# Normalisation stage: shift and scale weights loaded and multiplied ahead of the tokens, gate columns between the token groups, normalised rows written by POOL

## The chip, the cores and the metric

The kernel runs on one core of a Trainium2 chip. The metric is the device time of one execution in microseconds (us); lower is better. A time that is given is the median of several executions.

## The reference

The kernel computes two layers of a hybrid mixer over 1024 latent tokens and 256 context tokens of width 1024. The change touches only the head of each layer, the modulated layer norm:

```
shift, scale, gate = jnp.split(mod[:, None, :], 3, axis=-1)
shift_c, scale_c, gate_c = jnp.split(mod_c, 3, axis=-1)
u = _layer_norm(h) * (1.0 + scale) + shift
uc = _layer_norm(hc) * (1.0 + scale_c) + shift_c
z, xbc, dtr, q, k, v, gd, hp, gh = jnp.split(u @ w_in, IN_SPLITS, axis=-1)
```

Here `mod` and `mod_c` are rows of 3072 numbers, SiLU of a conditioning vector of 1024 times `w_ada` (1024 x 3072, fp32) plus a bias. Their first 1024 columns are the shift, the next the scale, the last the gate. The gate is only used at the layer's end, in the output stage. The rest of a layer (projections, a state-space scan, differential attention, long convolutions, the output projection with its own layer norm) stands after this stage and uses `u` and `uc`.

## The kernel before

`hybrid_backbone` runs its stages one after the other, and twice, once for each layer: `norm_stage`, `v_dt_stage`, `project_stage` and so on. Between two stages stands a barrier of all engines, so a stage ends with the last work of its slowest engine, and nothing of one stage lies beside another. Inside a stage each engine has a program of its own, written out by hand, and the order in it is fixed. Engines meet through semaphores.

`norm_stage` must leave two copies of the modulated and transposed tokens in SBUF: `u_hi`, rounded to fp32r, and `u_lo`, the remainder. Each is 128 partitions x 8 column blocks (k) x 1280 tokens. The tokens come as 10 tiles of 128 (2 of context, then 8 of latent tokens) in three groups: `batches` holds 2, 4 and 4 tiles. Item n is one column block of one group, 8 items for each group, 24 in all.

- SP (L204 to L221) issues all DMAs: the two conditioning vectors, all the tokens (`xn`: 1 MB, then twice 2 MB), the bias, and then `w_ada` in six column groups j of 512 columns, 2 MB each, into the two slots of `wa`. From j = 2 on it first waits until TensorE has multiplied group j - 2.
- PE (TensorE, L287 to L310) multiplies group j with the two conditioning vectors, 8 matmuls of 512 columns. The order is all six groups, then 16 small transposes that turn the shift and scale rows onto the partitions (`pT`), then the token transposes item by item into four PSUM slots (`px`), four 128 x 128 transposes for an item of 512 tokens.
- DVE (VectorE, L246 to L285) takes the first 6 token tiles through the layer norm (statistics, reciprocal, and the normalised rows by a `tensor_scalar` of 1024 columns, L265), then adds the bias to the six groups (L272), copies `pT` to `modT`, normalises the last 4 tiles, and at the end computes the remainder of each item (L284).
- ACT (ScalarE, L224 to L244) computes the SiLU, a square root for each tile, and then two activations for each item: `u_hi` (L240) and the same values in full fp32, `u` (L243), from which DVE subtracts.
- POOL (GpSimd) does nothing in this stage.

Only when `modT` is there can ACT begin with the items, and `modT` waits for all six groups, those of the gate too:

```
for j in range(NCH):
    pe.wait_ge(wada[j % 2], 16 * (j // 2 + 1))
    if j >= 2:
        pe.wait_ge(mod_ready, j - 1)
...
pe.wait_ge(mod_ready, NCH)
for k in range(2 * KD):
    mm = pe.transpose(pT[:, 2 * k:2 * k + 2], mod[:, k * P:(k + 1) * P], ident[0:2, 0:2])
```

## Time and profile before

| what | value |
|---|---|
| median of 3 runs | 4172.46 us (4168.78 to 4177.13) |
| the profiled execution, its own time | 4166.99 us |
| its span, first to last instruction | 4164.9 us |
| mean granted TensorE clock | 0.928 of full speed |
| busy: PE, DVE, ACT, POOL | 3522.2, 2521.2, 1081.6, 699.4 us |
| norm stage of layer 0, first DMA issue to last DVE work | 4.49 to 116.88 us |
| norm stage of layer 1, the same | 2228.86 to 2339.60 us |

The rows below are of four views. The timeline gives the start, the length, the engine, the line and the tiles of an instruction, and in brackets the idle time before it and what ended it. The table of windows gives a stretch, its length, the busy time of PE, PEld (weight loads), DVE, ACT and POOL in it, each with its number of instructions, then the granted TensorE clock (PEclk, 1.00 is 2.4 GHz and 0.50 is 1.2 GHz), the share of the DMA engines and their GB/s. The table of lines gives the number of instructions, their busy time in sum and the mean of one in ns. The table of DMA issues gives the count, the size and the us from issue to landing. Names that begin with `l_n_` belong to the norm stage of either layer.

### The profile page before, as it was taken

How to read it: one execution, taken by the hardware profiler on the slowest of the kernel's cores; microseconds unless marked ns; L12 is line 12 of the kernel's file. 1: busy time of each engine (PE TensorE's matmuls, PEld its weight loads, DVE VectorE, ACT ScalarE, POOL GpSimd, SP SyncE). 2: the span in 40 equal slices, each digit the busy share in tenths (PEclk: the TensorE clock that was granted, in tenths of full speed). 3: DMA queues.
4: the chain of work that ended last, by engine and by line, in shares of the span. 5: the costliest groups of instructions: out<-in, count | busy, mean ns of one | idle time of the engine just before them, and what ended most of it. 6: DMA issues, size and time to landing. Idle time of an engine off the chain costs nothing. (4 is left out here: it accounts for less than half of the span.)

```text
span 4164.9 us, 51062 instructions
## 1 busy us (share of the span) xinstructions
PE 3522.2 (85%) x19424; PEld 2889.8 (69%) x19424; DVE 2521.2 (61%) x5084; ACT 1081.6 (26%) x1861; POOL 699.4 (17%) x444
## 2 busy tenths in 40 slices
PE   5789999999778875996996788999999688859888
PEld 1677888888667774775782566788888577737577
DVE  3125677754279996765553324667773699967544
ACT  2212222222144443332110311222211344423310
POOL 0132333322100001210000122433343000012000
PEclk8899999999888997998998799999999799989999
DMA  4154223232253312334325145223231633123432
GB/s 174 55 142 144 94 85 97 81 101 74 72 162 97 89 35 74 122 98 150 118 81 187 36 115 163 88 81 97 81 100 62 188 84 84 40 100 105 134 115 71
DMA packets 414110, 424.53 MB, mean 102 GB/s; under 512 B 56908, under 2 KB 350540, under 8 KB 412710
## 3 DMA queue, kind: packets, MB, share of 16 engines
q1 hardware_dynamic: 368844, 319.55, 26.5%
q10 hardware_dynamic: 45024, 101.73, 6.9%
q8 instruction: 155, 2.54, 0.3%
q14 instruction: 87, 0.71, 0.1%
HBM read 288.28 MB, written 124.53 MB: 99 GB/s over the span
## 5 line engine op out<-in xcount | busy, mean ns | idle before, releaser
L665 PE MATMUL l_p_acc<-l_u_hi,l_p_w_hi 128*128 128x512 f32 (+1 forms) x2240 | 612.4, 376 | 49.5 <-POOL l_p_w_lo L580 37.0
L665 PE MATMUL l_p_acc<-l_u_hi,l_p_w_lo 128*128 128x512 f32 (+1 forms) x2240 | 593.5, 367 | 0.0
L665 PE MATMUL l_p_acc<-l_u_lo,l_p_w_hi 128*128 128x512 f32 (+1 forms) x2240 | 592.2, 367 | 0.0
L665 PEld LDWEIGHTS l_p_acc<-l_u_hi,l_p_w_hi 128*128 128x128 f32 x2240 | 390.4, 190 | 127.9 <-POOL l_p_w_lo L580 37.5
L665 PEld LDWEIGHTS l_p_acc<-l_u_hi,l_p_w_lo 128*128 128x128 f32 x2240 | 386.0, 189 | 72.4
L665 PEld LDWEIGHTS l_p_acc<-l_u_lo,l_p_w_hi 128*128 128x128 f32 x2240 | 385.8, 189 | 72.3
L578 POOL TENSOR_TENSOR l_p_w_hi<-l_p_wt,l_p_zero 128x1024 fp32r<-128x1024 f32 x104 | 207.7, 1997 | 983.2 <-PE l_p_acc L665 816.2
L1945 POOL TENSOR_TENSOR l_sd_xend<-l_sd_tok,l_sd_mine 128x512 f32<-128x512 f32 x80 | 85.6, 1072 | 1283.0 <-ACT l_sd_tok L1900 1282.2
L1402 PE MATMUL l_at_pS<-l_at_k_hi,l_at_q 128*128 128x512 f32 (+1 forms) x400 | 167.1, 418 | 147.2 <-ACT l_at_prob L1517 113.9
L580 POOL TENSOR_TENSOR l_p_w_lo<-l_p_wt,l_p_w_hi 128x1024 fp32r<-128x1024 f32 x104 | 271.0, 2606 | 8.2
L1586 DVE TENSOR_REDUCE l_at_nmax<-l_at_pS 128x1 f32<-128x1280 f32 (+1 forms) x144 | 197.1, 1369 | 81.7 <-PE l_at_pS L1403 78.7
L1517 ACT ACTIVATE l_at_prob<-l_at_pS,l_at_nmax 128x1280 f32<-128x1280 f32 (+1 forms) x144 | 177.4, 1232 | 249.5 <-DVE l_at_nmax L1586 249.5
L1402 PEld LDWEIGHTS l_at_pS<-l_at_k_hi,l_at_q 128*128 128x128 f32 x400 | 79.6, 199 | 186.3 <-ACT l_at_prob L1517 142.7
L876 DVE TENSOR_SCALAR l_p_cv<-l_p_stg,l_p_taps 128x1281 f32<-128x1281 f32 (+1 forms) x56 | 85.0, 1517 | 192.6 <-ACT l_p_stg L729 192.2
L822 DVE TENSOR_TENSOR l_p_R<-l_p_sw,l_p_rs 128x512 f32<-128x512 f32 x72 | 49.6, 689 | 228.7 <-PE l_p_sw L644 228.7
L1434 PE MATMUL l_at_pO<-l_at_v,l_at_mixT 128*128 128x128 f32 x1312 | 180.5, 299 | 7.6 <-ACT l_at_mixT L1524 4.5
L1434 PEld LDWEIGHTS l_at_pO<-l_at_v,l_at_mixT 128*128 128x128 f32 x1312 | 174.4, 215 | 10.1 <-issue 6.5
L878 DVE SCALAR_TENSOR_TENSOR l_p_cv<-l_p_stg,l_p_taps,l_p_cv 128x1281 f32<-128x1281 f32 (+1 forms) x56 | 150.8, 2692 | 2.0
L1524 ACT ACTIVATE l_at_mixT<-l_at_pT 128x512 f32<-128x512 f32 (+1 forms) x200 | 104.0, 520 | 181.3 <-PE l_at_pT L1418 181.3
L295 PE MATMUL l_n_pm<-l_n_wa,l_n_cond 128*2 128x512 f32 x192 | 88.0, 616 | 68.5 <-DMA l_n_wa<-w_ada 68.5
L1403 PE MATMUL l_at_pS<-l_at_k_lo,l_at_q 128*128 128x512 f32 (+1 forms) x400 | 144.0, 367 | 0.0
L643 PE MATMUL l_p_sw<-l_p_R,l_p_late 128*128 128x128 f32 x528 | 107.4, 286 | 34.0 <-DVEq L815 34.0
(324 smaller groups left out, 7051.2 us busy)
## 6 DMA issues: line engine op xcount, KB each, us to landing
l_p_wt<-w_in SPq DMA_DIRECT2D x104, 512.0 KB, 3.9
l_n_wa<-w_ada SPq DMA_DIRECT2D x12, 2048.0 KB, 8.2
xbc_d<-l_p_fin ACTq DMA_DIRECT2D x32, 640.0 KB, 2.9
kf_d<-l_p_R SPq DMA_DIRECT2D x72, 256.0 KB, 3.6
l_o_oT<-o_d SPq DMA_DIRECT2D x18, 1024.0 KB, 6.7
l_at_K<-kf_d SPq DMA_DIRECT2D x64, 256.0 KB, 2.9
l_o_rows<-w_out SPq DMA_DIRECT2D x32, 512.0 KB, 4.6
qk_d<-l_p_late ACTq DMA_DIRECT2D x12, 1280.0 KB, 4.8
```

The costliest lines, as they stand in the source:

```text
L295: mm = pe.matmul(pm[0:2, (j % 2) * BANK:(j % 2 + 1) * BANK], cond[:, k], wa[:, j % 2, k], start=(k == 0), stop=(k == KD - 1))
L578: pool.tensor_tensor(w_hi[:, m % 2], wt[:, m % 2], zero[:].unsqueeze(2).to_broadcast([P, KD, P]), ALU.add).then_inc(w_rounded, 1)
L580: pool.tensor_tensor(w_lo[:, m % 2], wt[:, m % 2], w_hi[:, m % 2], ALU.subtract).then_inc(w_split, 1)
L643: pe.matmul(out, mats[:, 4 * k + 2 * e], R[:, k, 0, cols], start=True, stop=False)
L665: mm = pe.matmul(acc[:, a:a + w], (w_hi, w_lo)[wp][:, m % 2, k], (u_hi, u_lo)[up][:, k, t0 + c:t0 + c + w], start=(k == n == 0), stop=(k = ...
L878: dve.scalar_tensor_tensor(cv[:, lo:], stg[:, lo:T + 1], taps[:, 0, tile:tile + 1], cv[:, lo:], ALU.mult, ALU.add).then_inc(conv_step, 1)
L1402: pe.matmul(out, q_s[:, s, m, q * P:(q + 1) * P], k_hi[:, s, m, c:c + w], start=True, stop=False)
L1403: mm = pe.matmul(out, q_s[:, s, m, q * P:(q + 1) * P], k_lo[:, s, m, c:c + w], start=False, stop=True)
L1434: mm = pe.matmul(pO[:, 0:P], mixT[:, kt], v_s[:, h % 2, kt], start=(kt == 0), stop=(kt == keys(q) // P - 1))
L1517: act.activation(prob[:, (2 * n + m) % 3, 0:keys(q)], pS[:, m * T:m * T + keys(q)], ACT.Exp, bias=nmax[:, n % 2, m:m + 1], accum_out=sums[ ...
L1524: act.activation(mixT[:, 4 * b:4 * b + w // P].rearrange("p a b -> p (a b)"), pT[:, 0:w], ACT.Copy).then_inc(turned_copied, 1)
L1586: dve.tensor_reduce(nmax[:, n % 2, m:m + 1], pS[:, m * T:m * T + keys(q)], AX.X, ALU.max, negate=True).then_inc(maxed, 1)
```

## The change

The weight loads now come first, and the tokens between them. The first 2 MB group of `w_ada` is loaded in two halves, and there are three weight slots (`WS` = 3) instead of two. The first four groups (`FRONT`, the shift and scale columns) come before the small transposes. Groups 4 and 5, the gate columns, are multiplied between the token groups. The statistics are taken for a whole group of tiles with one square root and one reciprocal, and POOL writes the normalised rows. For the items with odd n, DVE and no longer ACT computes `u` from PSUM (L318).

```diff
+    FRONT = 2 * D // GW
+    WS = 3
...
-                for j in range(NCH):
-                    if j >= 2:
-                        sp.wait_ge(mod_mm, j - 1)
-                    sp.dma_start(wa[:, j % 2], w_ada[:, j * GW:(j + 1) * GW].rearrange("(k p) n -> p k n", p=P)).then_inc(wada[j % 2], 16)
+                load_wada(0)
                 sp.dma_start(ba[:, :], b_ada.partition_broadcast(2)).then_inc(bada, 16)
+                load_wada(1)
+                load_h(0)
+                load_wada(2)
+                load_h(1)
+                load_wada(3)
+                load_h(2)
+                for j in range(FRONT, NCH):
+                    load_wada(j)
...
             @block.scalar
+                def turned(n):
+                    b, k = items[n]
+                    scale, shift = affine(n)
+                    act.wait_ge(xT_ready, n + 1)
+                    act.activation(u_hi[:, k, cols(b)], x_of(n), ACT.Identity, scale=scale, bias=shift).then_inc(hi_ready, 1)
+                    if n % 2 == 0:
+                        if n >= 4:
+                            act.wait_ge(lo_ready, n - 3)
+                        act.activation(u[:, n % 4, 0:width(b)], x_of(n), ACT.Identity, scale=scale, bias=shift).then_inc(u_act, 1)
+                for b, t in enumerate(batches):
+                    act.wait_ge(var_ready, b + 1)
+                    act.activation(mv[:, 2, t[0]:t[-1] + 1], mv[:, 1, t[0]:t[-1] + 1], ACT.Sqrt).then_inc(std_ready, 1)
+                    if b == 1:
+                        act.wait_ge(modT_ready, 1)
+                        for n in range(KD):
+                            turned(n)
+                for n in range(KD, len(items)):
+                    turned(n)
+            @block.gpsimd
+                for b, tiles in enumerate(batches):
+                    pool.wait_ge(rstd_ready, b + 1)
+                    for t in tiles:
+                        pool.tensor_scalar(xn[:, t], xn[:, t], mv[:, 0, t:t + 1], mv[:, 3, t:t + 1], ALU.subtract, ALU.mult).then_inc(xn_ready, 1)
...
             @block.vector
+                def remainders(b):
+                    for n in range(KD * b, KD * (b + 1)):
+                        k = items[n][1]
+                        dve.wait_ge(hi_ready, n + 1)
+                        if n % 2:
+                            scale, shift = affine(n)
+                            dve.tensor_scalar(u[:, n % 4, 0:width(b)], x_of(n), scale, shift, ALU.mult, ALU.add).then_inc(u_dve, 1)
+                            dve.wait_ge(u_dve, n // 2 + 1)
+                        else:
+                            dve.wait_ge(u_act, n // 2 + 1)
+                        dve.tensor_tensor(u_lo[:, k, cols(b)], u[:, n % 4, 0:width(b)], u_hi[:, k, cols(b)], ALU.subtract).then_inc(lo_ready, 1)
+                statistics(0)
                 dve.wait_ge(bada, 16)
+                modulation(0)
+                modulation(1)
+                statistics(1)
+                modulation(2)
+                modulation(3)
                 dve.wait_ge(modT_mm, 1)
                 dve.tensor_copy(modT[:].rearrange("p a b -> p (a b)"), pT[:, 0:4 * KD]).then_inc(modT_ready, 1)
+                dve.wait_ge(modT_ready, 1)
+                remainders(0)
+                statistics(2)
+                modulation(4)
+                remainders(1)
+                modulation(5)
+                remainders(2)
...
             @block.tensor
+                pe.wait_ge(mod_ready, FRONT)
                 for k in range(2 * KD):
                     mm = pe.transpose(pT[:, 2 * k:2 * k + 2], mod[:, k * P:(k + 1) * P], ident[0:2, 0:2])
                 mm.then_inc(modT_mm, 1)
+                turn(0)
+                modulation(4)
+                turn(1)
+                modulation(5)
+                turn(2)
```

SP's queue at the stage's start, before; `l_n_xn` is the tokens, `l_n_wa` the weights:

```order
L209 DMA l_n_xn<-ctx 128x2x1024
L212 DMA l_n_xn<-x 128x4x1024 x2
L213 DMA l_n_ba<-b_ada 2x3072
L218 DMA l_n_wa<-w_ada 128x8x512 x2
L218 DMA l_n_wa<-w_ada 128x8x512 [waits l0_n_mod_mm] x4
```

The same place, now:

```order
L229 DMA l_n_wa<-w_ada 128x4x512
L230 DMA l_n_wa<-w_ada 128x4x512
L243 DMA l_n_ba<-b_ada 2x3072
L232 DMA l_n_wa<-w_ada 128x8x512
L237 DMA l_n_xn<-ctx 128x2x1024
L232 DMA l_n_wa<-w_ada 128x8x512
L237 DMA l_n_xn<-x 128x4x1024
L232 DMA l_n_wa<-w_ada 128x8x512 [waits l0_n_mod_mm]
L237 DMA l_n_xn<-x 128x4x1024
L232 DMA l_n_wa<-w_ada 128x8x512 [waits l0_n_mod_mm] x2
```

5 MB of tokens stood ahead of the first weights; now three weight groups and two token groups stand ahead of the first load that waits for TensorE, and the last 2 MB of tokens behind it.

PE's program around the small transposes (`l_n_pT`), before; `l_n_pm` is a weight group, `l_n_px` an item's transposes:

```order
L295 MATMUL l_n_pm<-l_n_wa,l_n_cond 2x512 [waits l0_n_mod_ready,l0_n_wada1]
L295 MATMUL l_n_pm<-l_n_wa,l_n_cond 2x512 x7
L299 MATMUL l_n_pT<-ident,l_n_mod 128x2 [waits l0_n_mod_ready]
L299 MATMUL l_n_pT<-ident,l_n_mod 128x2 x15
L308 MATMUL l_n_px<-ident,l_n_xn 128x128 [waits l0_n_xn_ready]
```

The same place, now, from the small transposes to the second token group:

```order
L374 MATMUL l_n_pT<-ident,l_n_mod 128x2 [waits l0_n_mod_ready]
L374 MATMUL l_n_pT<-ident,l_n_mod 128x2 x15
L359 MATMUL l_n_px<-ident,l_n_xn 128x128 [waits l0_n_xn_ready]
L359 MATMUL l_n_px<-ident,l_n_xn 128x128 x7
...
L359 MATMUL l_n_px<-ident,l_n_xn 128x128 [waits l0_n_u_dve,l0_n_hi_ready]
L359 MATMUL l_n_px<-ident,l_n_xn 128x128
L348 MATMUL l_n_pm<-l_n_wa,l_n_cond 2x512 [waits l0_n_mod_ready,l0_n_wada1]
L348 MATMUL l_n_pm<-l_n_wa,l_n_cond 2x512 x7
L359 MATMUL l_n_px<-ident,l_n_xn 128x128 [waits l0_n_u_act,l0_n_hi_ready,l0_n_xn_ready]
L359 MATMUL l_n_px<-ident,l_n_xn 128x128 x3
```

Two of the six weight groups moved behind the small transposes, one of them into each gap between token groups, where they hold up the next group's transposes.

## Rows read from the trace of the kernel before

**Rows 1.** Windows, both norm stages: busy us and instructions, clock, DMA
```profile
4.49:116.88 112.39, 66.68 (x192) 22.52 (x192) 44.15 (x91) 33.53 (x61) 0.00 (x0) 0.84 0.45 159
2228.86:2339.60 110.74, 64.22 (x192) 21.68 (x192) 44.16 (x91) 33.53 (x61) 0.00 (x0) 0.73 0.46 162
```

**Rows 2.** Timeline of SP, layer 0: start, us, engine, line, out<-in
```profile
4.49 0.38 SPq L207 DMA_DIRECT2D l_n_cond<-c_ctx  x1
7.82 51.60 SPq L218 DMA_DIRECT2D l_n_wa<-w_ada  x6
```

**Rows 3.** Timeline of TensorE, norm stage of layer 0
```profile
27.36 16.54 PE L295 MATMUL l_n_pm<-l_n_wa,l_n_cond 128*2 128x512 f32 x32 [27.36 <-DMA l_n_wa<-w_ada]
67.61 7.03 PE L295 MATMUL l_n_pm<-l_n_wa,l_n_cond 128*2 128x512 f32 x16 [0.71 <-DMA l_n_wa<-w_ada]
75.41 1.14 PE L299 MATMUL l_n_pT<-ident,l_n_mod 2*128 2x2 f32 x16 [0.77 <-DVE l_n_mod L272]
100.07 1.12 PE L308 MATMUL l_n_px<-ident,l_n_xn 128*128 128x128 f32 x4 [0.22 <-ACT l_n_u L243]
```

**Rows 4.** Timeline of VectorE, norm stage of layer 0
```profile
10.92 1.28 DVE L254 BATCH_NORM_STATS2 l_n_st<-l_n_xn 128x6 f32<-128x512 f32 x2 [10.92 <-DMA l_n_xn<-ctx]
12.24 0.21 DVE L257 BATCH_NORM_AGGREGATE l_n_mv<-l_n_st 128x2 f32<-128x12 f32 x1
37.16 0.68 DVE L272 SCALAR_TENSOR_TENSOR l_n_mod<-l_n_pm,l_n_ba 2x512 f32<-2x512 f32 x1 [8.70 <-PE l_n_pm L295]
74.67 0.68 DVE L272 SCALAR_TENSOR_TENSOR l_n_mod<-l_n_pm,l_n_ba 2x512 f32<-2x512 f32 x1 [7.05 <-PE l_n_pm L295]
116.19 0.69 DVE L284 TENSOR_TENSOR l_u_lo<-l_n_u,l_u_hi 128x512 fp32r<-128x512 f32 x1 [0.65 <-ACT l_n_u L243]
```

**Rows 5.** DMA issues of the stretch 7.7 to 8 us
```profile
l_n_wa<-w_ada SPq DMA_DIRECT2D x1, 2048.0 KB, 19.4
```

**Rows 6.** Timeline of all engines, layer 1, the first weight group
```profile
2251.60 10.74 PE L295 MATMUL l_n_pm<-l_n_wa,l_n_cond 128*2 128x512 f32 x21 [36.17 <-DMA l_n_wa<-w_ada]
2260.31 0.68 DVE L272 SCALAR_TENSOR_TENSOR l_n_mod<-l_n_pm,l_n_ba 2x512 f32<-2x512 f32 x1 [7.60 <-PE l_n_pm L295]
```

**Rows 7.** Timeline of ScalarE, norm stage of layer 0
```profile
87.27 0.55 ACT L240 ACTIVATE l_u_hi<-l_n_px,l_n_modT 128x256 fp32r<-128x256 f32 x1
94.46 0.87 ACT L240 ACTIVATE l_u_hi<-l_n_px,l_n_modT 128x512 fp32r<-128x512 f32 x1
115.01 1.08 ACT L243 ACTIVATE l_n_u<-l_n_px,l_n_modT 128x512 f32<-128x512 f32 x1
```

**Rows 8.** Lines by shape, VectorE: count, busy us and mean ns, idle before
```profile
L284 DVE TENSOR_TENSOR l_u_lo<-l_n_u,l_u_hi 128x256 fp32r<-128x256 f32 x16 | 6.8, 426 | 6.8 <-ACT l_n_u L243 6.8
L764 DVE TENSOR_SCALAR l_p_R<-l_p_sw,l_p_R 64x512 f32<-64x512 f32 x8 | 6.4, 801 | 13.8 <-ACT l_p_R L681 7.4 <-PE l_p_sw L600 4.8 <-ACT l_p_hid L681 1.5
L764 DVE TENSOR_SCALAR l_p_R<-l_p_sw,l_p_R 64x256 f32<-64x256 f32 x2 | 1.1, 534 | 1.5 <-ACT l_p_R L681 0.8 <-ACT l_p_hid L681 0.8
```

**Rows 9.** Windows in the norm stage of layer 1, TensorE's clock
```profile
2302.00:2303.00 1.00, 0.00 (x0) 0.00 (x0) 1.00 (x3) 0.00 (x0) 0.00 (x0) 0.79 0.00 0
2320.00:2322.00 2.00, 1.21 (x8) 0.84 (x8) 1.20 (x2) 2.00 (x5) 0.00 (x0) 1.00 0.00 0
2322.00:2324.00 2.00, 1.00 (x5) 0.49 (x4) 0.88 (x2) 2.00 (x5) 0.00 (x0) 0.77 0.00 0
```

**Rows 10.** Lines by shape, POOL
```profile
L580 POOL TENSOR_TENSOR l_p_w_lo<-l_p_wt,l_p_w_hi 128x1024 fp32r<-128x1024 f32 x104 | 271.0, 2606 | 8.2
L975 POOL CAST l_v_wv_hi<-l_v_wv 128x512 fp32r<-128x512 f32 x16 | 9.8, 613 | 673.5 <-DMA l_v_wv<-w_in 673.5
```

**Rows 11.** Timeline of all engines, projection stage of layer 0
```profile
377.65 0.44 DVE L766 TENSOR_SCALAR l_p_R<-l_p_R 64x512 f32<-64x512 f32 x1
377.89 2.46 POOL L580 TENSOR_TENSOR l_p_w_lo<-l_p_wt,l_p_w_hi 128x1024 fp32r<-128x1024 f32 x1
378.13 2.51 DVE L768 TENSOR_SCALAR l_p_R<-l_p_R 64x512 f32<-64x512 f32 x1
```

155 lines of the change are left out of this document (77 added, 78 removed).

## The prediction

> **What bounds the kernel now.** I read the table of windows first. The two norm stages are 112.4 and 110.7 us long [rows 1], 223 of 4165 us, and in neither is any engine busy for more than 67 us, nor the DMA for more than 0.46 of the time. Barriers stand at both ends, so what such a stage loses in length the kernel loses too. The chain of waits is of no use here, since it shows only the last stage. The timelines show three parts in a row. First, tokens stand ahead of the weights: TensorE starts at 27.36 us [rows 3], though the first DMA was issued at 4.49 [rows 2]. Second, six weight groups pass one by one until the bias of the last at 74.67 [rows 4]. Third, after `modT`, ACT starts at 87.27 behind four normalisations and runs without a pause to the last activation at 115.01 [rows 7]; the last remainder ends at 116.88 [rows 4]. The change goes at all three.
>
> **The loads.** The first MB of tokens is there at 10.92 [rows 4]; the first weight group, 6.29 MB further, lands 19.4 us after 7.82 [rows 2, 5], at 27.2. That is 386 GB/s, 5.4 us for 2 MB. In the new order, with the first half group where the context tokens were, landings would be: first halves 10.9 and 13.6, group 1 at 19.1, context 21.8, group 2 at 27.2, latent tokens 32.7, group 3 at 38.1, latent tokens 43.5, groups 4 and 5 at 49.0 and 54.4. Group 3 is issued once group 0 is multiplied. Behind this wait on SP stand the last tokens and both gate groups. The queue has work up to 32.7, so a wait until some 21 us costs nothing.
>
> **TensorE's first part.** A weight group takes 7.03 us at full clock [rows 3], 8.7 in layer 1 as the first one after a pause (2251.60 to 2260.31, [rows 6]) and 9.8 in layer 0 (27.36 to 37.16, [rows 3, 4]). So: group 0 from 10.9 to 20.7, group 1 to 27.7, group 2 to 34.8. Group 3 waits for its load until 38.1. By then TensorE has idled 3.3 us; in an idle stretch of layer 1 the granted clock was already on its way from 2.4 to 1.2 GHz (0.79 in the third us, [rows 9]). I take 8.7: done at 46.8. From the start of a bias addition to that of the transposes are 0.74 us, the transposes take 1.14 [rows 3, 4], and a short copy 0.2 (an estimate): `modT` at 48.9, where it was at 76.8. VectorE is free for it: the second group's statistics, 8 times 0.64 plus 4 times 0.24 [rows 4], plus 0.8 for root and reciprocal, run from 32.7 to 39.7.
>
> **The first token group.** ACT needs 0.45 us for an activation of 256 columns (16 between 87.27 and 94.46) and 0.66 for one of 512 (31 between 94.46 and 115.01) [rows 7]. A pair of items had four, and now has three: 1.35 or 1.99 us. VectorE has two remainders, 0.43 or 0.69 [rows 4, 8], and the new `u` from PSUM: the trace's nearest form, two scalar operands from PSUM, takes 0.53 and 0.80 [rows 8]. With 0.04 between instructions that is 1.51 or 2.30 us for a pair, so VectorE sets the pace. The group ends at 48.9 + 1.1 + 4 x 1.51 = 56.0. TensorE has its last transposes of the group at 53.1, because they wait for `u` of item 3.
>
> **Gate group 4 and the second token group.** Its weights are there. Behind transposes I take the slow start, 8.7: 53.1 to 61.8. Meanwhile VectorE takes the last statistics, 56.0 to 62.8. ACT's last square root now stands ahead of the second group's activations, and they wait for it, until 62.7; TensorE's first transposes are ready then too, so this new wait costs nothing beyond gate group 4. VectorE adds the bias of group 4 and begins its remainders at 64.35. Unhindered, `u` of item 11, for which the group's last transposes wait, would end 5.5 us after ACT's start, at 68.2.
>
> **POOL beside VectorE.** From 62.8 POOL normalises four tiles. No POOL instruction of this form is in the trace. Bounds: 1.0 us, a little under two casts of 512 columns (0.61 each), and 2.6, the two-input form of 1024 columns [rows 10]. I take 1.3, the cast being the nearest row with one tensor input. When POOL ran beside a VectorE `tensor_scalar` that otherwise takes 0.44, this one lasted 2.51 and ended just after POOL's [rows 11]: one waits for the other's whole instruction. The remainders have two SBUF inputs. If they wait too, alternating with POOL: item 8's ends at 66.1 instead of 65.0, item 9's at 68.1, item 10's at 70.1, `u` of item 11 at 70.9, 2.7 us late. I take this. The Trainium skill (SBUF — State Buffer, "Who interferes with whom") says that a VectorE instruction with two SBUF inputs contends with a GpSimd instruction that reads SBUF, and that whichever comes second fully blocks. The rows show it for a one-input instruction only; without the lock for two inputs each stage would be 2.7 us shorter.
>
> **Gate group 5 and the end.** The last transposes of the second group end at 72.0; group 5 then takes 8.7, to 80.7. This step lies wholly on the path: ACT and VectorE have run dry by 77. Transposes do not hold the clock: in layer 1 it was 1.00 through 2320 to 2322 and 0.77 in the next 2 us, with nothing but transposes on TensorE [rows 9]. The Trainium skill (TensorE: Matmul & The Clock Gate, Part 4, PE-mode transpose) says that the full clock does not engage for transposes. The 1.00 speaks against the word, the fall for its drift; by the rule groups 4 and 5 start slow, with the clock held they take 7.03. First transposes of the last group (4 take 1.1, [rows 3]) and ACT's start: 81.5. End: 81.5 + 1.65 + 4 x 2.30 = 92.3. POOL has been done since 69.4. The store of the gate rows (issued at 81.4) ends in the cover of this.
>
> **Sum.** Layer 0: 116.9 - 92.3 = 24.6. Layer 1 runs the same course, since its path from 27 us on hangs on loads: 110.7 - (92.3 - 4.5) = 22.9. Together 47.5 us: 4166.99 - 47.5 = 4119.5 for the profiled execution, whose own time is 5.5 below the median of 4172.46. From the median it would be 4125; I say 4124. The stages behind begin, as before, with TensorE cold; I see nothing there that moves.
>
> **Rivals.**
> 1. Clock held and no lock. Group 3 ends at 45.2, `modT` 47.3; first group to 54.4; gate 4 ends 58.5, the statistics at 61.2; second group's transposes 67.8, gate 5 at 74.8, end 86.4. Gain 30.5 + 28.8 = 59.3: 4113. For: 7.03 in the steady groups. Against: rows 9 and 11. Chance 0.12.
> 2. POOL at 2.4 us with the lock, and slow starts of 9.8 throughout: 2.0 and 3.3 us more in each layer, gain 37: 4135. For: 9.8 was measured once. Against: the cast. Chance 0.17.
> 3. Slower: POOL becomes the bound. Its ten instructions form one chain from 25.9 us (context statistics), and the last items cannot begin before it ends: 25.9 + 10 X + 11.7. At X = 7.9 us the stage is as long as before; at 8.5 it gives +6 and +7 us, 4185. For: the form is not in the trace. Against: none of POOL's 1024-column rows is over 2.6 in the mean. Chance 0.04.
> 4. It does not do what it says: TensorE runs at the lower clock through every group, some 14 us for each (twice 7.03), six in series plus the token groups: 10.9 + 6 x 14 + 3 + 7 + 9 + 11 = 125 us. Against: the clock came back within the first group in both layers, or it would not have ended in 8.7 and 9.8. What is left of it, one or two groups slow throughout, eats part of the gain: 5 to 7 us for each, at most some 25 in both layers, 4150; and at the end a no change. Chance 0.03 for a result within 0.2%.
>
> **Numbers.** The forecast itself has 0.64, its own range 4117 to 4131. The rivals 1 and 2 are cases of the same sign, so the range goes over both, with 5 us for the spread of the runs: 4107 to 4142. A change of under 0.2%, 8 us, can't be told from none: faster 0.93, same 0.03, slower 0.04.
>
> **What would show it.** First weight matmul near 11 us; `modT` near 49; two gaps in ACT's activations, one of some 8 us before item 8 and one of some 6 before item 16; remainders of over 1 us while POOL is busy; last remainder near 92. Wrong if `modT` is past 55 (loads), if POOL's instruction exceeds 3 us, or if the stages behind change by over 5 us.

## The result, and the profile after

The changed kernel takes 4105.52 us (median of 4 executions, 4095.83 to 4109.27), beside it the kernel before 4173.78 (4 executions): ratio 0.984, 95% interval 0.9823 to 0.9857. That is 1.6% faster, in the direction that was forecast, but by more: 18.5 us below the forecast of 4124 and 1.5 below the range's lower end of 4107. The profiled execution took 4105.7 us, its span 4103.9, the mean clock 0.935 (0.928 before). One execution of a later kernel, `split`, took 4929.32 us at a mean granted clock of 0.683, where its others had 0.933 to 0.936; nothing recorded says why, and the times given for that kernel leave it out.

Both norm stages, in the table of windows, now from the first DMA issue to that of the stage behind. The columns are those of [rows 1]:

```profile
4.45:89.25 84.80, 59.55 (x192) 18.05 (x192) 40.69 (x79) 25.35 (x42) 38.17 (x10) 0.92 0.58 211
2196.90:2280.60 83.70, 59.20 (x192) 18.00 (x192) 40.42 (x79) 25.34 (x42) 38.19 (x10) 0.87 0.58 214
```

By the same marks the two stages took 113.18 and 111.52 us before. They are 28.4 and 27.8 us shorter, 56.2 together, where 47.5 were forecast. The ten instructions of POOL are 38.2 us, 3.8 each. That lies outside the bounds of 1.0 to 2.6 that I had set.

TensorE's timeline, layer 0, to be laid beside [rows 3]:

```profile
11.18 4.91 PE L365 MATMUL l_n_pm<-l_n_wa,l_n_cond 128*2 128x512 f32 x8 [11.18 <-DMA l_n_wa<-w_ada]
...
38.54 8.32 PE L348 MATMUL l_n_pm<-l_n_wa,l_n_cond 128*2 128x512 f32 x16 [3.51 <-DMA l_n_wa<-w_ada]
...
54.23 9.01 PE L348 MATMUL l_n_pm<-l_n_wa,l_n_cond 128*2 128x512 f32 x16
...
69.81 7.03 PE L348 MATMUL l_n_pm<-l_n_wa,l_n_cond 128*2 128x512 f32 x16
77.90 1.97 PE L359 MATMUL l_n_px<-ident,l_n_xn 128*128 128x128 f32 x16 [1.07 <-POOL l_n_xn L285]
```

TensorE starts at 11.18 us instead of 27.36, and group 3 waits for its load until 38.54 (forecast 10.9 and 38.1). Gate group 4 is slow, gate group 5 is not, and the last token group waits at the end not for gate group 5 but 1.07 us longer, for POOL. POOL and VectorE in the same stage (with [rows 4]):

```profile
62.28 15.56 POOL L285 TENSOR_SCALAR l_n_xn<-l_n_xn,l_n_mv 128x1024 f32<-128x1024 f32 x4 [8.19 <-DVE l_n_mv L305]
```

```profile
48.81 0.19 DVE L332 COPY l_n_modT<-l_n_pT 128x32 f32<-128x32 f32 x1 [1.24 <-PE l_n_pT L374]
50.40 1.38 DVE L322 TENSOR_TENSOR l_u_lo<-l_n_u,l_u_hi 128x256 fp32r<-128x256 f32 x1 [1.39 <-ACT l_n_u L266]
...
84.86 0.81 DVE L318 TENSOR_SCALAR l_n_u<-l_n_px,l_n_modT 128x512 f32<-128x512 f32 x1
85.70 1.29 DVE L322 TENSOR_TENSOR l_u_lo<-l_n_u,l_u_hi 128x512 fp32r<-128x512 f32 x2
86.91 0.81 DVE L318 TENSOR_SCALAR l_n_u<-l_n_px,l_n_modT 128x512 f32<-128x512 f32 x1
87.75 0.69 DVE L322 TENSOR_TENSOR l_u_lo<-l_n_u,l_u_hi 128x512 fp32r<-128x512 f32 x1
```

`modT` is there at 49.0, as forecast. The last remainder ends at 88.44 instead of 92.3. The clock, in windows of layer 0:

```profile
54.00:58.00 4.00, 4.00 (x7) 0.59 (x6) 3.93 (x9) 1.01 (x3) 0.10 (x1) 0.50 0.01 2
66.00:73.00 7.00, 4.95 (x21) 1.93 (x21) 6.90 (x11) 6.00 (x9) 7.00 (x3) 1.00 0.00 0
```

Group 4 begins at 1.2 GHz; before it TensorE had made two pauses of 0.61 and 1.56 us between the first group's transposes. Through the transposes of the second token group and into gate group 5 the clock stays at 2.4 GHz, against what [rows 9] had shown and what I took. Layer 1 runs the same course, but for group 3, which is at full clock there:

```profile
2231.11 7.03 PE L348 MATMUL l_n_pm<-l_n_wa,l_n_cond 128*2 128x512 f32 x16 [3.56 <-DMA l_n_wa<-w_ada]
...
2245.57 9.01 PE L348 MATMUL l_n_pm<-l_n_wa,l_n_cond 128*2 128x512 f32 x16
...
2261.16 7.03 PE L348 MATMUL l_n_pm<-l_n_wa,l_n_cond 128*2 128x512 f32 x16
2269.26 1.97 PE L359 MATMUL l_n_px<-ident,l_n_xn 128*128 128x128 f32 x16 [1.06 <-POOL l_n_xn L285]
```

Last, two remainders that were held up, and the POOL instruction beside the second, each from a timeline cut narrowly about it:

```profile
66.86 0.92 DVE L322 TENSOR_TENSOR l_u_lo<-l_n_u,l_u_hi 128x512 fp32r<-128x512 f32 x1
```

```profile
69.81 4.27 POOL L285 TENSOR_SCALAR l_n_xn<-l_n_xn,l_n_mv 128x1024 f32<-128x1024 f32 x1
...
71.19 0.85 DVE L322 TENSOR_TENSOR l_u_lo<-l_n_u,l_u_hi 128x512 fp32r<-128x512 f32 x1
```

A free one takes 0.69. POOL's four instructions of this group begin at 62.28, 66.05, 69.81 and 74.07.

### The profile page after: what moved, and what is told of

It reads as the page before. It is cut to its first block and busy times, and to the rows that moved or that the text cites. A ratio compares the mean times of both kernels' runs of the same rounds, so it can differ in the third digit from the quotient of the medians.

```text
span 4103.9 us, 51032 instructions
## 1 busy us (share of the span) xinstructions
PE 3507.0 (85%) x19424; PEld 2879.6 (70%) x19424; DVE 2514.7 (61%) x5060; ACT 1064.3 (26%) x1823; POOL 779.5 (19%) x464
## 5 line engine op out<-in xcount | busy, mean ns | idle before, releaser
L2014 POOL TENSOR_TENSOR l_sd_xend<-l_sd_tok,l_sd_mine 128x512 f32<-128x512 f32 x80 | 85.5, 1071 | 1285.9 <-ACT l_sd_tok L1969 1285.1
L285 POOL TENSOR_SCALAR l_n_xn<-l_n_xn,l_n_mv 128x1024 f32<-128x1024 f32 x20 | 76.4, 3829 | 491.8 <-DVE l_n_mv L305 491.8
L2055 DVE SCALAR_TENSOR_TENSOR l_sd_state<-l_sd_state,l_sd_mine,l_sd_pS 128x64 f32<-128x64 f32 x576 | 116.5, 275 | 30.5 <-PE l_sd_pS L1889 30.5
```

The costliest lines, as they stand in the source:

```text
L2055: last = dve.scalar_tensor_tensor(state[:, s, d, nxt, h], state[:, s, d, c, h], mine[:, s, 1, c, d, h:h + 1], pS[:, d * BANK + h * HD:d * ...
```

## The experiments

"Stages" are the lengths of the two norm stages in the profiled execution, between the marks above; "the others" is the sum of the remaining eleven stages of that execution. For the kernel before they are 113.2 and 111.5, and 3935.7, for the changed kernel 84.8 and 83.7, and 3931.0. Ratios are to the kernel before, timed on the same chip.

### Rows on VectorE (dve_rows)

```diff
-            @block.gpsimd
-                        pool.tensor_scalar(xn[:, t], ..., ALU.subtract, ALU.mult)
+                    for t in batches[b]:          # VectorE, behind the reciprocal
+                        dve.tensor_scalar(xn[:, t], ..., ALU.subtract, ALU.mult)
```

> The normalised rows go back from POOL to VectorE (ten tensor_scalar of 1024 columns, behind each group's reciprocal); all else is the changed kernel, whose norm stages are 84.8 and 83.7 us long. POOL took 3.78 us for each row block, where VectorE took 0.81 in the kernel before. Theory A, POOL is slow but hidden: VectorE gets 3.3 us more ahead of the second group's remainders, of which 2.5 lie in a wait, so gate group 5 ends some 0.8 us later; in exchange the last group no longer waits 1.07 us for POOL, and the first remainder is no longer held up by 0.95. Stages 84 to 85 us, total within 3 us of the changed kernel. Theory B, POOL's rows are worth their VectorE time: +3.3 us or more for each stage, total +6 to +7 us.

Measured: 4104.05 us (4095.15 to 4109.36), ratio 0.9836 (0.9816 to 0.9856); stages 84.6 and 83.6. As theory A said, the length hardly changes. But the equal length hides effects that cancel. TensorE, layer 0:

```profile
66.66 1.07 PE L355 MATMUL l_n_px<-ident,l_n_xn 128*128 128x128 f32 x8 [2.70 <-ACT l_u_hi L262]
68.71 1.09 PE L355 MATMUL l_n_px<-ident,l_n_xn 128*128 128x128 f32 x4 [0.98 <-DVE l_n_u L314]
69.73 8.08 PE L344 MATMUL l_n_pm<-l_n_wa,l_n_cond 128*2 128x512 f32 x16
77.75 1.97 PE L355 MATMUL l_n_px<-ident,l_n_xn 128*128 128x128 f32 x16
```

The wait for POOL before the last group is gone. In its place TensorE pauses for 2.70 us while VectorE writes rows, its transposes are slow after that (1.09 for four instead of 0.63), and gate group 5 takes 8.08 instead of 7.03. It begins at the same time as before, 69.73, only because gate group 4 ended 2.1 us earlier: no POOL instruction held up the first remainder, so group 4 began 0.8 us earlier, and it took 7.72 instead of 9.01. From this run alone POOL looks free; the run "split" below shows that it is not.

### Gate groups ahead of all tokens (gates_first)

```diff
-                for j in range(1, FRONT):         # TensorE
+                for j in range(1, NCH):
                     modulation(j)
...
-                modulation(4)                     # and 5, behind turn(0) and turn(1)
...
+                statistics(2)                     # VectorE, ahead of the small transposes
+                modulation(4)
+                modulation(5)
```

> All six weight groups ahead of the small transposes again, the statistics of the last token group between groups 3 and 4, and then the three token groups without a pause; loads, POOL's rows and the split of u stay as in the changed kernel. Theory A, the gate groups lie on TensorE's path wherever they stand, since ACT and VectorE run dry behind each: group 5 ends near 62, ACT starts near 64.6 instead of 49.3, but 24 items follow without a pause (5 + 8.3 + 8.3 us), end near 87.5, stages 83 to 84.5 us, total within 3 us of the changed kernel. Theory B, the gate columns between the token groups are hidden there and this is what the change gains by: stages 94 to 99 us, total +20 to +30 us.

Measured: 4108.45 us (4103.28 to 4110.53), ratio 0.9847 (0.9831 to 0.9863), stages 85.5 and 86.8. TensorE in layer 0:

```profile
49.58 13.89 PE L345 MATMUL l_n_pm<-l_n_wa,l_n_cond 128*2 128x512 f32 x32 [2.00 <-DMA l_n_wa<-w_ada]
```

The two groups now run in one piece before `modT`, in layer 0 at full clock; in layer 1 the first of them begins behind a pause of 3.55 us and takes 8.72. ScalarE starts 16.6 us later but isn't interrupted any more. The total is 2.9 us above the changed kernel's, within the 3 us of theory A; its stages of 83 to 84.5 us are missed by 1.0 and 2.3. Where the gate groups stand on TensorE is worth 0.7 to 3.1 us for a stage. They are on the path in either place, 14 to 16 us of it.

### Only the load order undone (tokens_first)

```diff
-                load_wada(0)
-                sp.dma_start(ba[:, :], ...)
-                load_wada(1)
-                load_h(0)
...
+                load_h(0)
+                load_h(1)
+                load_h(2)
+                sp.dma_start(ba[:, :], ...)
+                load_wada(0)                      # then 1, 2, 3
```

> Only the order of the loads is undone: all tokens ahead of the weights, the rest as in the changed kernel (three slots, four groups ahead of the small transposes). Theory A, the first weight matmul sets everything behind it: it moves from 11.2 to 27.2 us, the four groups then run without the 3.5 us wait for group 3, ACT starts at 59.4 instead of 49.3, stages 94 to 95 us, total +19 to +21 us. Theory B, the stage is set by VectorE and POOL once the gate groups are out of the way: under +8 us in total.

Measured: 4119.57 us (4115.46 to 4129.28), ratio 0.9879 (0.9859 to 0.9899), stages 93.5 and 93.8. TensorE:

```profile
24.61 6.07 PE L365 MATMUL l_n_pm<-l_n_wa,l_n_cond 128*2 128x512 f32 x8 [24.61 <-DMA l_n_wa<-w_ada]
...
61.80 9.67 PE L348 MATMUL l_n_pm<-l_n_wa,l_n_cond 128*2 128x512 f32 x16
```

TensorE starts 13.4 us later, of which 8.7 come out at the stage's end: with all weights waiting, it no longer stands still before group 3. So the load order is worth 8.7 and 10.1 us, about a third of the 56. The stages are near what theory A expected (94 to 95). The first matmul came 2.6 us earlier than it said, and the total is 14.1 us above the changed kernel's, not 19 to 21: the other stages of this profile, 3925.6, are the shortest of all.

### ScalarE computes every u (act_u)

```diff
-                    if n % 2 == 0:
-                        if n >= 4:
+                    if n >= 4:
                             act.wait_ge(lo_ready, n - 3)
...
-                            dve.tensor_scalar(u[:, n % 4, 0:width(b)], x_of(n), scale, shift, ALU.mult, ALU.add)
```

> ACT computes u of all 24 items again, VectorE only the remainders; the rest as in the changed kernel. An item of 512 columns then takes 1.33 us instead of 1.03, one of 256 columns 0.90 instead of 0.62. Theory A, only the last token group is on the path with its whole length: VectorE finishes the first group 1 us later, the last group takes 10.7 instead of 8.3 us, stages 86.5 to 88 us, total +5 to +8 us. Theory B, every item counts: 8 x 0.28 + 16 x 0.30 = 7 us for each stage, total +14 us. Of the clock: the slower transposes of the second group leave TensorE's clock at 2.4 GHz as now (group 5 takes 7.03 us), or it falls as between 2320 and 2324 us of the kernel before (group 5 takes 8.7).

Measured: 4111.8 us (4109.37 to 4116.97), ratio 0.9855 (0.9836 to 0.9873), stages 88.7 and 89.2. The clock of layer 0 in a window within the second token group, and the gate group behind it:

```profile
66.00:68.00 2.00, 1.63 (x7) 1.29 (x8) 1.33 (x2) 2.00 (x4) 2.00 (x2) 0.53 0.00 0
```

```profile
69.76 8.61 PE L342 MATMUL l_n_pm<-l_n_wa,l_n_cond 128*2 128x512 f32 x16
```

An item takes 1.34 us instead of 1.03, so the split of `u` brings 0.31 us for an item of 512 columns. The stages are 3.9 and 5.5 us longer, about 1 us more than theory A allowed, the total 6.3, as it said; part of the difference is the clock (group 3 took 8.72 and 9.84). In layer 0 the clock fell during the transposes, as in [rows 9]; in layer 1 of the same execution gate group 5 took 7.03. So both courses are to be had with only transposes on TensorE.

### The changed and the old kernel again (after_again, before_again, before_third, before_fourth)

> The changed kernel itself, unaltered. Theory A (what the seven stages outside the two norm stages take differs by several us from one execution to the next): the norm stages repeat within 0.5 us (84.8 and 83.7), the sum of the others differs from 3930.9 by 1 to 5 us. Rival B (the change itself moves the other stages, 3935.6 before, 3930.9 after): the sum repeats within 1 us.

> The kernel before, unaltered, for one more profile. Theory A (spread of executions): norm stages 113.2 and 111.5 us again within 0.5, the others 3925 to 3940 and different from the 3935.6 of the first profile. Rival B: 3935.6 within 1 us, so the 4.7 us between this and the changed kernel's 3930.9 would belong to the change.

> The kernel before, unaltered, for a third profile. The order of instructions outside the norm stages is the same in both kernels. Theory A (the projection stage of layer 0 differs between the two kernels in every execution: 916.8 and 922.3 us in two profiles of the kernel before, 908.8 to 913.5 in eleven of the changed kernel and its variants): over 914 us again. Rival B (chance: it depends on how VectorE's and POOL's instructions happen to fall on each other): anywhere from 909 to 922, at least one of the two repeats within 913.5.

> The same once more. Theory A: the projection stage of layer 0 is over 914 us in this profile too. Rival B: one of the two repeats lies within 908 to 913.5.

Measured: the changed kernel 4103.71 us (4099.55 to 4105.82), ratio 0.9837 (0.982 to 0.9853), stages 86.7 and 85.8, the others 3927.1. My "repeats within 0.5 us" was wrong: it was 2 us off, and the old kernel's stages below differ by up to 2 us too. TensorE and POOL in layer 0:

```profile
38.36 9.96 PE L348 MATMUL l_n_pm<-l_n_wa,l_n_cond 128*2 128x512 f32 x16 [3.45 <-DMA l_n_wa<-w_ada]
...
54.65 8.66 PE L348 MATMUL l_n_pm<-l_n_wa,l_n_cond 128*2 128x512 f32 x16
...
69.67 7.03 PE L348 MATMUL l_n_pm<-l_n_wa,l_n_cond 128*2 128x512 f32 x16
79.82 1.97 PE L359 MATMUL l_n_px<-ident,l_n_xn 128*128 128x128 f32 x16 [3.12 <-POOL l_n_xn L285]
```

```profile
63.17 16.60 POOL L285 TENSOR_SCALAR l_n_xn<-l_n_xn,l_n_mv 128x1024 f32<-128x1024 f32 x4 [9.22 <-DVE l_n_mv L305]
```

Group 3 took 9.96 instead of 8.32, and the wait for POOL 3.12 instead of 1.07.

The old kernel's single profiles: times 4170.11, 4169.65 and 4169.24 us; stages 111.9 and 111.4, 112.8 and 112.9, 113.2 and 110.9; the others 3940.4, 3936.6 and 3937.8. Its projection stage of layer 0 took 922.3, 917.0 and 919.3 us, after 916.8 the first time. In the changed kernel it was 913.3 and 912.2. No repeat comes down to 913.5: this difference is no chance, though nothing in this stage was changed.

### What POOL's instruction costs (pool_forms)

```diff
+                        if b == 0:
+                            pool.tensor_scalar(xn[:, t], xn[:, t], mv[:, 0, t:t + 1], None, ALU.subtract)
...
+                            pool.tensor_scalar(xn[:, t], xn[:, t], mv[:, 3, t:t + 1], None, ALU.mult)
+                        elif b == 1:
+                            pool.tensor_scalar(xn[:, t, 0:BANK], ..., ALU.subtract, ALU.mult)
+                            pool.tensor_scalar(xn[:, t, BANK:D], ..., ALU.subtract, ALU.mult)
```

> The changed kernel with POOL's normalisation in other forms: the two context tiles as a subtraction and a multiplication apart (1024 columns, one pointer scalar each), the four tiles of group 1 as halves of 512 columns with two pointer scalars, the last four as they were. Theory A (3.78 us is a price for each column and each of the two operations): one-scalar instructions 1.8 to 2.2 us, halves 1.9. Rival B (a fixed price for the form or for its pointers): halves 3.5 us and more, one-scalar ones either 3.5 or more or about 1.2, as the cast. POOL's work stays in the cover of other engines up to some 62 us, so the total may be 0 to 4 us longer under both.

Measured: 4100.38 us (one execution). POOL, the tile's instructions: ns of the shortest, the median and the longest:

```profile
L292 POOL TENSOR_SCALAR l_n_xn<-l_n_xn,l_n_mv x4: 2077/2080/2082, 38.8 to 51.2; 128x512 f32<-128x512 f32 x4
...
L287 POOL TENSOR_SCALAR l_n_xn<-l_n_xn,l_n_mv x2: 2844/2847/2850, 25.8 to 31.6; 128x1024 f32<-128x1024 f32 x2
```

```profile
L295 POOL TENSOR_SCALAR l_n_xn<-l_n_xn,l_n_mv x4: 3780/3782/4287, 61.8 to 73.6; 128x1024 f32<-128x1024 f32 x4
```

1024 columns take 3.78 us and 512 take 2.08: 0.38 fixed and 3.3 ns a column. With one operation instead of two 1024 columns take 2.85. So it is a price by column, and the second operation with its pointer scalar is 0.93 of it. The halves are near what theory A said (1.9), the one-scalar instructions lie between the theories.

### One tile of each group on VectorE (split)

```diff
-                    for t in tiles:
+                    for t in tiles[:3]:           # POOL
...
+                rows(2)                           # VectorE, the fourth tile, behind statistics(2)
```

> The changed kernel, but the fourth tile of each latent group is normalised by VectorE (0.75 us each) and POOL has three (11.3 us instead of 15.1 to 16.6). Theory A (the last group's transposes wait for POOL: in the two profiles of the changed kernel 1.07 and 3.12 us after gate group 5 was done with, in layer 0): they now start when gate group 5 ends, at 76.9 us if it takes 7.03; each stage is 0.5 to 1.5 us shorter than 84.8 and 83.7 (2 to 3 less than 86.7 and 85.8), total 1 to 5 us below the changed kernel. Rival B (gate group 5 sets this start in any case): with a row's tile taken by VectorE nothing changes or the stage gets 0.8 us longer, total within 2 us.

Measured: stages 83.5 and 83.7, the others 3936.0. TensorE in layer 0:

```profile
38.41 10.01 PE L355 MATMUL l_n_pm<-l_n_wa,l_n_cond 128*2 128x512 f32 x16 [3.46 <-DMA l_n_wa<-w_ada]
...
54.72 8.69 PE L355 MATMUL l_n_pm<-l_n_wa,l_n_cond 128*2 128x512 f32 x16
...
69.75 7.03 PE L355 MATMUL l_n_pm<-l_n_wa,l_n_cond 128*2 128x512 f32 x16
76.71 1.97 PE L368 MATMUL l_n_px<-ident,l_n_xn 128*128 128x128 f32 x16
```

This execution had the same slow groups as after_again (10.01 and 8.69 beside 9.96 and 8.66), so the two can be laid side by side: there the last token group began at 79.82, here at 76.71, and the stage is 3.2 us shorter, the wait for POOL that is gone. Theory A holds in the stage. In the total it doesn't show: 4107.54 us (median of 3 executions, 4103.87 to 4109.5), ratio 0.9851 (0.9831 to 0.9871). In the profiled execution the other stages were at their long end.

### No pause before group 3 (warm), and a half load taken back (after_whole)

```diff
+                        if j == 2 and k == KD - 1:
+                            pe.wait_ge(mod_ready, 1)
+                            for i in range(4):
+                                pe.matmul(pm[0:2, 0:BANK], cond[:, i], wa[:, 2, i], start=True, stop=True)
```

```diff
-                        sp.dma_start(wa[:, 0, 0:4], rows[:, 0:4]).then_inc(wada_first, 16)
-                        sp.dma_start(wa[:, 0, 4:8], rows[:, 4:8]).then_inc(wada[0], 16)
+                        sp.dma_start(wa[:, 0], rows).then_inc(wada[0], 16)
```

> The changed kernel, with four matmuls more (3.5 us, their result is overwritten) in TensorE's wait for the load of group 3, so that it does not pause there. Theory A (group 3 lost its 1.3 to 2.9 us over 7.03 to that pause, in some executions): group 3 takes 7.03 us in both layers, modT comes at 46 to 47.6 us, but the stage is shorter only by what POOL and the slow start of gate group 4 leave of it: 0 to 1.5 us. Rival B (the pause has nothing to do with it): group 3 again takes 8.3 to 10 us in one of the layers, no change. In either case the total differs by less than 4 us.

> The changed kernel with its first weight group loaded in one piece: TensorE starts when 2 MB are there instead of 1, near 13.8 us instead of 11.2 in layer 0, and then needs only what comes behind; group 3 waits for its load until 38.5 us in any case, so theory A (this half load is worth nothing as long as group 3 waits): norm stages 84 to 87 us as before, TensorE's pause before group 3 gets 1 to 2.7 us shorter. Rival B: the start comes through to the end, 2 to 3 us more in each. For the projection stage of layer 0: theory A3 wants 916 us or more here, otherwise 908 to 913.5.

Measured, warm: 4100.24 us (4097.06 to 4115.0), ratio 0.9845 (0.9824 to 0.9866), stages 83.3 and 83.3; after_whole: 4101.98 us (one execution), stages 83.5 and 83.2. TensorE in layer 0, first of warm (18 matmuls, 16 of them group 3), then of after_whole:

```profile
37.32 8.12 PE L352 MATMUL l_n_pm<-l_n_wa,l_n_cond 128*2 128x512 f32 x18
```

```profile
13.63 5.08 PE L364 MATMUL l_n_pm<-l_n_wa,l_n_cond 128*2 128x512 f32 x8 [13.63 <-DMA l_n_wa<-w_ada]
...
37.98 7.03 PE L347 MATMUL l_n_pm<-l_n_wa,l_n_cond 128*2 128x512 f32 x16 [2.11 <-DMA l_n_wa<-w_ada]
```

Group 3 runs at full clock in both layers of both kernels. After its pause of some 3.5 us it took 7.03 us in four cases (all in layer 1) and 8.3 to 10.0 in twelve, over the eight profiles of kernels with this pause. The half load buys a start 2.5 us earlier, and all of it is lost again before group 3: loaded in one piece the stages are no longer. Here the pause before group 3 is 2.1 to 2.3 us, and the clock stayed up.

### The gate matmuls woven in (woven, woven_warm)

```diff
+                after_item = [3, 5, 7] + list(range(8, 21))
...
+                        if n in after_item:       # one of the 16 gate matmuls behind this item
+                            mm = pe.matmul(pm[0:2, ...], cond[:, kk], wa[:, j % WS, kk], start=(kk == 0), stop=(kk == KD - 1))
...
+                bn(2, batches[2][:2])             # VectorE, before modulation(3)
+                rows(1, batches[1])
```

> The 16 matmuls of the gate groups stand one by one behind single items of the token transposes instead of in two blocks; the statistics of the last group stand in VectorE's waits before modT; VectorE writes the rows of group 1 and one tile of group 2, POOL only the context tiles and three of the last group. Theory A (after modT the stage is bound by VectorE's remainders, and the two blocks of gate matmuls are what interrupts them): the last remainder ends near 78 us in layer 0 instead of 88.4, each norm stage is 9 to 10 us shorter than in the changed kernel, the total 18 to 20 us below it. Rival B (a gate matmul between transposes delays the next item by its own 0.44 us or more, so that TensorE becomes the bound at over 2.3 us a pair): stages 4 to 6 us shorter, total 6 to 12 us below. Rival C (the clock falls with matmuls spread thinly, transposes and gate matmuls both at 1.2 GHz): no gain or a loss.

> The woven kernel with the same four matmuls. Theory A (from modT on TensorE sets the end of the woven stage, at 1.54 us for an item with its gate matmul): group 3 takes 7.03 instead of 8.7 us in both layers, and the whole of these 1.7 us comes out at the end: stages 75.5 instead of 77.2 and 77.0, total 2 to 4 us below the woven kernel, at 4084. Rival B (VectorE, with some 41 us of work from the second group's statistics on, sets the end): the stages stay at 76.5 to 77.5 and VectorE has no more waits of 0.7 us between the items; total within 1 us.

Measured: woven 4087.11 us (4083.64 to 4094.29), ratio 0.9802 (0.9787 to 0.9818), stages 77.2 and 77.0; woven_warm 4085.57 us (4081.4 to 4086.32), ratio 0.9801 (0.9786 to 0.9815), stages 75.6 and 75.7. TensorE and ScalarE of woven, in a steady stretch:

```profile
63.37 1.02 PE L400 MATMUL l_n_pm<-l_n_wa,l_n_cond 128*2 128x512 f32 x2
64.32 0.66 PE L393 MATMUL l_n_px<-ident,l_n_xn 128*128 128x128 f32 x4
```

```profile
65.01 0.78 ACT L262 ACTIVATE l_u_hi<-l_n_px,l_n_modT 128x512 fp32r<-128x512 f32 x1 [0.76 <-PE l_n_px L393]
```

TensorE has no pause: 0.95 for a gate matmul and 0.59 for an item's transposes, 1.54 an item, while ScalarE waits 0.76 us for it at every other item. Rival B's mechanism is right: TensorE becomes the bound, at 3.07 us a pair of items, over its 2.3. Yet 7.6 and 6.7 us are gained, between the two forecasts. The warm variant confirms the bound: group 3 takes 7.03 instead of 8.72, and 1.6 and 1.3 us come out at the end. Between these two the medians are 1.5 us apart, within their spread. Both beat the changed kernel: 16.6 us for woven beside after_again in the same series. That is the gain of the whole edit, the rows and statistics that moved included; how much is the weaving alone wasn't tried.

### What shortens the projection stage (before_slots, before_stats, before_halves)

```diff
-        wa = sb(nc, ctx, tag + "wa", [P, 2, KD, GW])
+        wa = sb(nc, ctx, tag + "wa", [P, 3, KD, GW])   # before_slots
```

```diff
-                for t in range(TT):
-                    act.activation(mv[:, t, 2:3], mv[:, t, 1:2], ACT.Sqrt)
+                for b, tiles in enumerate(batches):    # before_stats
+                    act.activation(mv[:, 2, tiles[0]:tiles[-1] + 1], mv[:, 1, tiles[0]:tiles[-1] + 1], ACT.Sqrt)
```

```diff
+                    if j == 0:                         # before_halves
+                        sp.dma_start(wa[:, 0, 0:4], rows[:, 0:4]).then_inc(wada[0], 16)
+                        sp.dma_start(wa[:, 0, 4:8], rows[:, 4:8]).then_inc(wada[0], 16)
```

> The kernel before with memory for three weight slots and three PSUM slots, as the changed kernel has it, but with nothing else changed; the third is not used. Theory A1 (the placement of the norm stage's tiles in memory carries over to the stages behind): projection stage of layer 0 at 908 to 913.5 us. Theory A2 (it is something else in the norm stage) and rival B: 914 us and more, or anywhere from 909 to 922. The norm stages stay at 111 to 113.5 us in any case.

> The kernel before with one part of the change alone: the statistics for a whole group of tiles, one square root and one reciprocal for each, the normalised rows still on VectorE. In the norm stage, four normalisations stand between modT and the first item; their batch saves some 3 square roots and waits of 0.8 us: stages 110 and 108.5 instead of 113 and 111. Theory A2 (the number of instructions that VectorE and ScalarE pass through in the norm stage shifts what comes behind): projection stage of layer 0 at 908 to 913.5 us, as in the changed kernels. Otherwise 916 to 923, as in five profiles of the kernel before.

> The kernel before with its first weight group loaded in two halves, so that it issues one DMA more in each norm stage, as the changed kernel does. Norm stages 111 to 113.5 us as before. Theory A3 (how the transfers of the later stages are spread over the queues depends on the number of DMAs before them): projection stage of layer 0 at 908 to 913.5 us. Otherwise 916 to 923.

Measured (one execution each): 4172.38, 4159.06 and 4175.9 us; projection stage of layer 0 920.6, 918.8 and 921.0; after_whole, which takes the DMA out of the changed kernel, 911.6. None of the three, alone, is the cause. The statistics in batches shorten the norm stages to 107.5 and 107.6, by 5.7 and 3.9 us, more than the 3 expected. TensorE at the place where the two kernels part, 610 us into the projection stage, before and now, each with the window of 4 us that begins there:

```profile
820.96 0.55 PE L643 MATMUL l_p_sw<-l_p_R,l_p_late 128*128 128x128 f32 x2 [4.33 <-DVEq L815]
...
820.96:824.96 4.00, 4.00 (x20) 3.96 (x21) 3.81 (x6) 0.00 (x0) 0.00 (x0) 0.57 0.02 4
```

```profile
792.72 0.46 PE L712 MATMUL l_p_sw<-l_p_R,l_p_late 128*128 128x128 f32 x2 [1.98 <-DVEq L884]
...
792.72:796.72 4.00, 4.00 (x28) 3.75 (x29) 3.81 (x6) 0.00 (x0) 0.00 (x0) 1.00 0.54 135
```

The order of instructions is the same in both. From the stage's first DMA issue (at 211.00 and 183.48 us) TensorE runs dry after 605.6 us before and 607.3 now, and goes on at 610.0 and 609.2. Its pause is 2.35 us longer before, and behind it the clock is the lower one, 0.57 against 1.00. Measured against the first profile of the changed kernel, each of the seven profiles with the old norm stage falls back here by 3.7 to 7.3 us, with pauses of 4.1 to 5.2. Eleven of the twelve with the new one fall back by 0.4 at most, with pauses of 1.7 to 2.3; dve_rows, with 3.34, by 2.9.

One step further back, 22 us earlier, VectorE, for which TensorE waits here, waits for a store of its results (`kf_d`), before and now:

```profile
798.22 0.76 DVE L1059 TENSOR_TENSOR l_p_R<-l_p_Tm 128x256 f32<-128x256 f32 x2 [2.22 <-DMA kf_d<-l_p_R]
```

```profile
770.40 0.76 DVE L1128 TENSOR_TENSOR l_p_R<-l_p_Tm 128x256 f32<-128x256 f32 x2 [0.29 <-DMA kf_d<-l_p_R]
```

In the seven old profiles this wait is 1.95 to 3.19 us, in the twelve new ones 1.22 at most. ScalarE issues a store of 640 KB (`xbc_d`) beside it: from 0.6 us ahead of SP's last `kf_d` issue to 0.5 behind it in the old ones, 0.8 to 1.0 behind it in the new ones. That the two stores get in each other's way is likely but wasn't tried, and what puts the engines at another distance from each other in a stage behind a barrier stays open.

## Why the prediction was wrong by its size

The mechanism and the direction were right, and so was the shape: two gaps, `modT` at 49, the gate groups wholly on the path. The size was not. For the pair of profiled executions the sum was 47.5 us and 61.3 were measured; the missing 13.8 are 8.7 in the norm stages, 4.8 in the others and 0.3 outside both. The rest of the 18.5 are the 4.5 us that I added to come from the profiled execution to the median: the changed kernel's profile lies at its median, that of the kernel before below its own. Layer 1 gained 1.1 us more over its forecast than layer 0, as group 3 ran at full clock there. The terms that failed were the hold of POOL on VectorE, gate group 5's slow start, the pace of the last group and the zero for the stages behind. Point by point, layer 0:

- **The loads**: right. 11.18 and 38.54 for 10.9 and 38.1.
- **TensorE's first part**: right in sum (`modT` 49.0 for 48.9). Group 3's slow start is no fixed term, though: 7.03 in layer 1, 9.96 in after_again.
- **Gate group 4**: 9.01 for 8.7, begun 1.1 us late, mostly since POOL, which by my price would have been done, held up VectorE's first remainder by 0.95. ScalarE starts item 8 at 63.86 instead of 62.7. The statistics ended at 62.19 (forecast 62.8), so their wait cost nothing, as said.
- **The lock: failed, the first large error.** I took the whole instruction of POOL as the hold, 2.7 us in the second token group. POOL's instructions are three times as long as I took them, and yet the hold is 0.4 us there. The remainder begun 0.08 us into a POOL instruction took 1.38 instead of 0.43, one begun 0.81 us into it 0.92 instead of 0.69; those begun later took their usual time, but for one of 0.85, begun 1.38 us into a POOL instruction that was itself 0.5 us longer. In each case the hold ends about 1.0 us into POOL's instruction, or 1.5 into the longer one. Gate group 5 began at 69.81, not 72.0. The hold is thus a part of POOL's instruction only: over two thirds of it lie beside VectorE's undisturbed. The word "fully blocks" of the Trainium skill (SBUF — State Buffer, "Who interferes with whom") is too strong for this pair. [rows 11], from which I took the whole instruction, is another pair: there POOL has two SBUF inputs and VectorE one. Such a POOL instruction does hold up a VectorE instruction with two SBUF inputs until about its end. In the projection stage of the kernel before one that takes 0.42 alone took 2.62:

```profile
801.54 2.62 DVE L1055 TENSOR_TENSOR l_p_R<-l_p_Tm 128x256 f32<-128x256 f32 x1
```

```profile
801.42 2.47 POOL L580 TENSOR_TENSOR l_p_w_lo<-l_p_wt,l_p_w_hi 128x1024 fp32r<-128x1024 f32 x1
```

- **Gate group 5: failed, the second.** 7.03 us where I took 8.7. I had generalised [rows 9]. With 0.6 us of transposes at a time, two items to a pair of 2.05 us, the clock was 1.00 throughout. It fell in act_u and dve_rows, and in one layer each of tokens_first and pool_forms. Over nine profiles with this group in the second gap, two layers each, it took 7.03 us 13 times and 8.1 to 9.2 five times; group 4 took 7.03 four times and 7.7 to 9.7 fourteen times. Here the full clock didn't have to engage, and it held. In the kernel before it engaged: in layer 1 TensorE had nothing but transposes from 2311.05 us on, first at 0.50, then partly, and from 2320 to 2322 [rows 9] wholly at full clock:

```profile
2311.00:2318.00 7.00, 5.97 (x23) 3.87 (x24) 3.51 (x9) 7.00 (x16) 0.00 (x0) 0.50 0.00 1
2318.00:2320.00 2.00, 1.61 (x7) 0.86 (x5) 0.69 (x1) 2.00 (x5) 0.00 (x0) 0.59 0.00 0
```

  The word of the Trainium skill that the full clock doesn't engage for transposes (TensorE: Matmul & The Clock Gate, Part 4, PE-mode transpose) isn't borne out.
- **POOL's price: outside my bounds.** 3.78 us, not 1.3, nor within 1.0 to 2.6. I took a cast of one operand as the nearest row; this form has two operations and two pointers. That POOL's instruction exceeds 3 us was one of my signs of being wrong. POOL was done at 77.84 instead of 69.4, and the last token group waited 1.07 us for it, 3.12 in after_again. That is the beginning of rival 3, which I put at X = 7.9 us for "as slow as before". POOL came to set the end from some 3.6 us on (76.84 less 62.28, by four), and it cost 1 to 3 us only. Gate group 5's earlier begin, its shorter time and this wait (-2.2, -1.7, +1.1) put ScalarE's start on the last group at 78.60 instead of 81.5.
- **The pace: failed, the third.** 2.05 us a pair, not 2.30; 1.0 us over the last group. I had added VectorE's durations and 0.04 between them. In the rows above two remainders take 1.29 together and 0.69 alone: consecutive instructions overlap by 0.09, and one that doesn't depend on the last starts before it ends. For ScalarE I had read the pace from first to last start ([rows 7]), and that one was right.
- **The stages behind**: I saw nothing there that would move. They are 4.8 us shorter in this pair of profiles. In seven profiles with the old norm stage (in three of them slightly changed) the sum is 3935.7 to 3943.9, in twelve with the new one 3925.6 to 3936.0, 9.6 us less in the mean, almost twice the 5 us that I gave as a sign of being wrong. 7.5 of this is the projection stage of layer 0 (919.4 and 911.9, 916.8 and more against 913.5 and less). That it is so is shown, also between executions on one chip. Where it arises is shown as far as the pause at 610 us. What carries it over a barrier stays open: the slots' memory, the batched statistics and the extra DMA, each alone, aren't it. The other parts weren't tried alone, nor was the moment at which the stage begins, which separates the profiles as well (204.9 to 211.4 us in the old ones, 175.0 to 191.0 in the new).

Of the rivals, 1 (clock held, no lock, 4113) came nearest. It had a chance of 0.12 from me, on the strength of a single stretch of [rows 9] and one collision in [rows 11]. Its nearness is in part luck: groups 3 and 4 did start slow in layer 0, the norm stages gave 56.2 us and not its 59.3, and the 4.8 us of the stages behind made up for it.

Taken back or put in alone, the load order is worth 18.7 us over both layers, the batched statistics 9.6 (on the kernel before), the split of `u` 9.4 and the place of the gate groups 3.8, together 41.5 of the 56.2, as far as such gains add. What is left wasn't tried alone.

## What to carry to other kernels

Read an engine's pace from first start to last start over a run of instructions, never from the sum of durations. A clock that fell once in the trace is not a fixed term for every pause; give it both values and let the range hold them. What a collision of one pair of instructions cost is no price for another pair: look how many tensor inputs each has. When an experiment that takes something away changes nothing, look whether two effects cancelled: only two executions with the same slow groups showed that POOL was on the path.
